# Reciprocal square roots of the mixers' norms: Ln and Exp on ScalarE replaced by Sqrt with VectorE's reciprocal, and by GpSimd's power

## The reference

```
def _l2_normalize(x):                      # RWKV keys per head of 64; GD queries and keys per head of 128
    return x * lax.rsqrt(jnp.sum(x * x, axis=-1, keepdims=True) + 1e-6)

y = ((y - mean) * lax.rsqrt(var + RW_LN_EPS)) * ln_g + ln_b      # RWKV output, per head of 64
o = _rms_norm(o, norm_g) * silu(zgate)                            # GD output, per head of 128
h = _rms_norm(h, norm_g) * sigmoid(o)                             # mLSTM output, per head of 128
```

## Time and profile before

| | us |
|---|---|
| median of three runs | 3327.88 |
| lowest, highest | 3312.94, 3331.92 |
| span of the profiled execution | 3333.3 |
| TensorE, VectorE, ScalarE, GpSimd busy | 3222.5, 2135.0, 1682.0, 610.8 |

### The profile page before, as it was taken

One profiled execution on the slowest core, in us unless ns is written; L12 is line 12 of the kernel. 1 busy time (PEld: TensorE's weight loads), 2 busy tenths in 40 slices (PEclk: granted clock), 3 DMA queues, 4 the chain that ended last, 5 costly groups with the idle time before them and its releaser, 6 DMA issues.

```text
span 3333.3 us, 51588 instructions
## 1 busy us (share of the span) xinstructions
PE 3222.5 (97%) x18431; PEld 2802.3 (84%) x18431; DVE 2135.0 (64%) x3426; ACT 1682.0 (50%) x2659; POOL 610.8 (18%) x521
## 2 busy tenths in 40 slices
PE   8999998999999999999999999999999999999998
PEld 7899897877888888888788998887878888888886
DVE  5775655776677777545568655556767777774554
ACT  5545544444655555444455565434455555554444
POOL 2000442342122212100000013324411222220000
PEclk9999997999999999999999998979999999999999
DMA  6666001113566666665556650011145665656654
GB/s 204 180 181 180 25 1 32 49 58 95 172 194 193 188 183 193 223 194 189 166 167 193 188 149 1 1 51 57 52 124 177 192 189 178 187 191 219 192 185 153
DMA packets 265208, 478.91 MB, mean 144 GB/s; under 512 B 17314, under 2 KB 81148, under 8 KB 264380
## 3 DMA queue, kind: packets, MB, share of 16 engines
q1 hardware_dynamic: 265020, 476.48, 46.4%
HBM read 474.32 MB, written 2.10 MB: 143 GB/s over the span
## 4 chain that ended last, share of the span: by engine, by line
PE 90%; DVE 5%; ACT 2%; issue 1%; DVEq 0%; ACTq 0%; POOL 0%; SPq 0%; DMA 0%; POOLq 0%
PE ps L625 89%; PE ps L629 1%; ACT L1223 1%; DVE wlo L1727 1%; DVE upair L1740 0%; ACT UA L1223 0%; DVE H L1759 0%; DVE AR L2128 0%; ACT XS L1223 0%; DVE TN L2149 0%; DVE TN L1786 0%; DVE rf L2163 0%; POOL H L562 0%; ACT whi L1223 0%; DVE XS L1776 0%
## 5 line engine op out<-in xcount | busy, mean ns | idle before, releaser
L1727 DVE TENSOR_TENSOR wlo<-ring,whi 128x1024 fp32r<-128x1024 f32 (+4 forms) x905 | 1086.3, 1217 | 693.8 <-ACT whi L1223 687.3
L625 PE MATMUL ps<-upair,whi 128*128 128x512 f32 x4032 | 1416.9, 396 | 5.8 <-DVE upair L1740 5.2
L1223 ACT ACTIVATE whi<-ring 128x1024 fp32r<-128x1024 f32 (+4 forms) x947 | 941.1, 1002 | 805.3 <-PE ps L625 752.8
L625 PE MATMUL ps<-upair,wlo 128*128 128x256 f32 x4032 | 1130.9, 280 | 0.0
L625 PEld LDWEIGHTS ps<-upair,whi 128*128 128x128 f32 x4032 | 757.4, 188 | 186.1 <-issue 5.9
L625 PEld LDWEIGHTS ps<-upair,wlo 128*128 128x128 f32 x4032 | 762.7, 189 | 0.3 <-issue 0.2
L625 PE MATMUL ps<-whi,upair 128*128 128x390 f32 (+2 forms) x1280 | 367.9, 364 | 0.0
L607 POOL TENSOR_TENSOR YB<-YB 128x1024 f32<-128x1024 f32 x22 | 125.2, 5691 | 837.9 <-DVE YB L1750 837.9
L625 PE MATMUL ps<-whi,ghi 128*128 128x512 f32 x704 | 274.4, 390 | 0.0
L625 PE MATMUL ps<-whi,glo 128*128 128x512 f32 x704 | 274.0, 389 | 0.0
L625 PE MATMUL ps<-wlo,ghi 128*128 128x512 f32 x704 | 273.9, 389 | 0.0
(11 more groups left out here) (304 smaller groups left out, 3802.6 us busy)
## 6 DMA issues: line engine op xcount, KB each, us to landing
ring<-in_w_up_dram SPq DMA_DIRECT2D x352, 512.0 KB, 3.8
ring<-in_w_down_dram SPq DMA_DIRECT2D x176, 512.0 KB, 4.2
ring<-in_w_in_dram SPq DMA_DIRECT2D x128, 384.0 KB, 3.5
ring<-in_w_out_dram SPq DMA_DIRECT2D x64, 512.0 KB, 3.8
ring<-in_w_ple_gate_dram SPq DMA_DIRECT2D x64, 512.0 KB, 4.1
ring<-in_w_in_dram SPq DMA_DIRECT2D x51, 512.0 KB, 4.4
ring<-in_w_in_dram SPq DMA_DIRECT2D x64, 390.0 KB, 3.5
ring<-in_w_in_dram SPq DMA_DIRECT2D x32, 396.0 KB, 3.4
```

Of the source, the lines that this page charges most:

```text
L625: return pe.matmul(o_, a, b, start=start, stop=stop, skip_group_check=True)
L1223: return act.activation(o_, i_, f, **kw)
L1727: v.tensor_tensor(wlo[:, slot % RING, :, 0:w], ring[:, slot % RING, :, 0:w], whi[:, slot % RING, :, 0:w].bitcast(F32), SUB).then_inc(S["lo ...
```

## The change

ScalarE takes no logarithm for a norm any more. For the RWKV keys it only copies the sums out of PSUM, at level 1, and signals `rw_rn` there; GpSimd adds epsilon and raises to the power -0.5 by a tensor_tensor with `ALU.pow` against a broadcast column of -0.5. The RWKV output norm goes to GpSimd wholly, which now waits for `rw_var`. For the GD keys ScalarE takes Sqrt, and VectorE the reciprocal of both 128x512 tiles, between its exponents and AR. For the GD and mLSTM outputs ScalarE takes Sqrt, VectorE the reciprocal of 128x4. `ready_roots` and `ready_exps` place table loads by hand: the set with Sqrt ahead of the wait for the mLSTM sums, the set with Exp behind the key norms' signal.

```diff
@@ GpSimd
+                def inverse_root(o_, i_, width, eps):
+                    pool.tensor_tensor(pst[:, 0:1], ident[:, 0:1], ident[:, 0:1], ALU.mult)
+                    pool.tensor_scalar(o_, i_, 1.0 / width, eps, ALU.mult, ALU.add)
+                    pool.drain()
+                    pool.tensor_tensor(o_, o_, epsb[:, 3:4].to_broadcast([P, o_.shape[-1]]), ALU.pow)
+                    pool.drain()
 ...
                     pool.wait_ge(S["rw_rn"], n + 1)
+                    inverse_root(ch[:, 3, :], ch[:, 3, :], 1, EPS)
                     pool.tensor_tensor(ch[:, 4, :], ch[:, 1, :], ch[:, 3, :], ALU.mult)
 ...
-                    pool.wait_ge(S["rw_rstd"], n + 1)
+                    pool.wait_ge(S["rw_var"], n + 1)
+                    inverse_root(st[:, 2, :], st[:, 1, :], 64, RW_LN_EPS)
                     pool.tensor_tensor(o4, o4, bc(st[:, 2, :], 64), ALU.mult)
@@ ScalarE
-            def rsqrt(o_, i_, scale, bias):
-                a(o_, i_, ACT.Ln, scale=scale, bias=bias)
-                act.drain()
-                return a(o_, o_, ACT.Exp, scale=-0.5)
+            def ready_roots():
+                act.preload_act_table_set("sqrt_and_friends")
+            def ready_exps():
+                act.preload_act_table_set("exp_and_friends")
+            def root(o_, i_, scale, bias):
+                return a(o_, i_, ACT.Sqrt, scale=scale, bias=bias)
 ...
-            def rw_norms(c, n, logs, exps, banks=(1, 5)):
-                if logs:
+            def rw_norms(c, n, sums, values, banks=(1, 5)):
+                if sums:
                     act.wait_ge(S["rw_ssq"], n + 1)
-                    a(ch[:, 3, :], ps[banks[0]][:, 0:T], ACT.Ln, bias=epsb[:, 0:1])
-                    if c > 1:
-                        act.wait_ge(S["rw_var"], n - 1)
-                        a(st[:, 2, :], st[:, 1, :], ACT.Ln, scale=1.0 / 64, bias=epsb[:, 1:2])
-                if exps:
-                    act.drain()
-                    a(ch[:, 3, :], ch[:, 3, :], ACT.Exp, scale=-0.5)
-                    if c > 1:
-                        a(st[:, 2, :], st[:, 2, :], ACT.Exp, scale=-0.5).then_inc(S["rw_rstd"], 1)
+                    a(ch[:, 3, :], ps[banks[0]][:, 0:T], ACT.Copy)
                     rc = rows["r_k"] + c
                     a(ch[:, 2, :], zrw[:, c, :], ACT.Copy, scale=par[:, rc:rc + 1])
                     act.drain().then_inc(S["rw_rn"], 1)
+                if values:
                     act.wait_ge(S["rw_vt"], n + 1)
 ...
-                def rw_rstd(n):
-                    act.wait_ge(S["rw_var"], n + 1)
-                    rsqrt(st[:, 2, :], st[:, 1, :], 1.0 / 64, epsb[:, 1:2]).then_inc(S["rw_rstd"], 1)
 ...
-                            else:
-                                rw_rstd(n - 1)
 ...
                     act.wait_ge(S["gd_ssq"], n + 1)
                     for j in range(2):
-                        a(mono(ewg[j], 2), ps[(7, 5)[j]][:, :], ACT.Ln, bias=epsb[:, 0:1])
-                    act.drain()
-                    for j in range(2):
-                        last = a(ewg[j], ewg[j], ACT.Exp, scale=-0.5)
+                        last = root(mono(ewg[j], 2), ps[(7, 5)[j]][:, :], 1.0, epsb[:, 0:1])
                     last.then_inc(S["gd_rn"], 1)
+                    ready_exps()
 ...
                         if src == "gd_us":
                             partial_out(ng, sg, 2)
+                            ready_roots()
                             act.wait_ge(S["ml_ss"], n + 1)
-                            rsqrt(st[:, 2, :], st[:, 1, :], 1.0 / P, epsb[:, 0:1]).then_inc(S["ml_rstd"], 1)
+                            root(st[:, 2, :], st[:, 1, :], 1.0 / P, epsb[:, 0:1]).then_inc(S["ml_rstd"], 1)
 ...
-                    rsqrt(st[:, 2, :], st[:, 1, :], 1.0 / P, epsb[:, 0:1]).then_inc(S["gd_rstd"], 1)
+                    root(st[:, 2, :], st[:, 1, :], 1.0 / P, epsb[:, 0:1]).then_inc(S["gd_rstd"], 1)
@@ VectorE
                 v.wait_ge(S[fam + "_rstd"], n + 1)
+                v.reciprocal(st[:, 2, :], st[:, 2, :])
+                v.drain()
                 v.tensor_tensor(OL, OL, bc(st[:, 2, :], P), MUL)
 ...
                     v.wait_ge(S["gd_rn"], n + 1)
+                    for j in range(2):
+                        v.reciprocal(mono(ewg[j], 2), mono(ewg[j], 2))
+                    v.drain()
                     for h in range(2):
```

More of the change, by code:

```diff
@@ L256, in trunk @@
             inv_tn1 inv_x inv_xs inv_q inv_t inv_tn inv_tq inv_tt0 inv_tt1 inv_th
-            rw_u rw_uf rw_state rw_s0 rw_pv2 rw_rf2 rw_u2 rw_uf2 rw_y rw_yc rw_var rw_rstd rw_done
+            rw_u rw_uf rw_state rw_s0 rw_pv2 rw_rf2 rw_u2 rw_uf2 rw_y rw_yc rw_var rw_done
             gd_sp gd_ln gd_gl gd_cum gd_cumc gd_exp gd_silu gd_sq gd_ssq gd_rn gd_vt gd_vtc gd_qk gd_kt gd_ktc gd_sc
@@ L437, in _ @@
             for dst, v in ((ones[:], 1.0), (one_h[:], 1.0), (ident[:], 0.0), (headones[:], 0.0), (prow, 0.0),
-                           (epsb[:, 0:1], EPS), (epsb[:, 1:2], RW_LN_EPS), (epsb[:, 2:3], 1.0)):
+                           (epsb[:, 0:1], EPS), (epsb[:, 1:2], RW_LN_EPS), (epsb[:, 2:3], 1.0), (epsb[:, 3:4], -0.5)):
                 pool.memset(dst, v)
@@ L1517, in _ @@
                     rw_pair(c, c < RC - 1)
-                rw_rstd(act.snap(L * RC + (RC - 1)))
                 def ml_pair(n2, lv):
```

## The result

| | us |
|---|---|
| median after | 3613.11 (3612.86 to 3623.09) |
| median before, measured beside it | 3329.9 (3312.94 to 3333.15) |
| ratio | 1.0871, 95% interval 1.0842 to 1.0900 |
| span of the profiled execution | 3611.1, against 3333.3 before |

The change makes the kernel 8.7% slower: +283 us, where +15 was forecast. The time lies far outside the range.

The account below looks back on a forecast made before the run. TensorE, busy 97% of the span, bounds the kernel. A layer, C 6.7 + D 6.9 + F 2.9 - B 3.0 - B's clock 5.0 - E 0.9 = +7.6; two, +15 on 3327.9: 3343 us, range 3325 to 3390.

Parts of the forecast that it names:

- A: Norms of the rwkv pairs moved to GpSimd: 13.7 us to spare, cost nothing if the wide power stays under 12 us.
- F: First rwkv pair's products: 3.8 us to spare, the added GpSimd chain costs +2.9 us a layer with the power at 5.7.
- rival 3: GpSimd's wide power is slow, costing later pairs too: 3375 us at a 15 us power, 3416 at 20; chance 0.23.
- B: Last rwkv pair: ScalarE's chain loses two loads and a Ln, -3.0 us; TensorE's clock stays up, -5.0 us, each layer.
- rival 2: TensorE's clock in the last rwkv pair falls all the same: 10 us more, 3353 us; chance 0.18.
- C: Round 0, GD key norms: two wide VectorE reciprocals, 3.3 us each, go on the path, +6.7 us a layer.
- Rivals 4 and 5: Round reciprocals: 4, streaming like ordinary operations, 3308 us, chance 0.06; 5, eight times ordinary per element, 3356 us, chance 0.07.
- D: Rounds 1 and 2: reciprocals outweigh saved loads, +2.7 us and +0.75 of clock each, +6.9 us a layer.
- E: End of round 2: VectorE's wait for ScalarE shortens, small reciprocals added, net -0.9 us a layer.
- Rest: Row-norm load behind the mixers, moved rw_var wait, last output norm and hand-placed loads: hidden or about where they were.
- Rival 6: Loads are still put before each Sqrt beside the hand-placed ones: hidden behind the reciprocals, 3343 us too; chance 0.04.

Follow-up runs that it names:

- experiment 3: Kernel before with only the RWKV output norms moved to GpSimd, with a power of 128x4; 3298.52 us, ratio 0.9921.
- experiment 6: Kernel of experiment 1 with each of VectorE's two wide reciprocals a round replaced by a product with a constant; 3312.33 us, ratio 0.9969.
- experiment 1: Changed kernel with the 128x256 power of the RWKV key norms replaced by a same-shape GpSimd product; 3339.73 us, ratio 1.0039.
- experiment 2: Kernel before with only the GD and mLSTM part of the change (Sqrt, VectorE reciprocals, hand-placed loads); 3357.64 us, ratio 1.011.

## Why the prediction was wrong, step by step

**A and F failed by the price of the wide power.** The prediction bounded it by 0.73 and 5.7 us, the engine's longest row of any kind, and took 5.7; it is 41.27. The longest row of another operation is no bound for an operation that the trace doesn't have, and the range went by it. With 5.7 us step A came out at nothing and F at 2.9 us a layer; measured, TensorE stands 26.4 to 27.8 us at the coefficient product of each of pairs 1 to 3, and the first pair starts 27.6 us late. The power was the only term with nothing comparable in the trace; that called for more than 0.23 on rival 3, and for an upper end of the range that doesn't stop at 17 us.

**Rival 3's mechanism was right, its two terms not quite.** Its rule (F grows as the power less 2.8 us, A costs three times what exceeds 12.7) gives 3353, 3422 and 3586 for powers of 10.7, 20.9 and 41.3 us; measured were 3363, 3464 and 3613. The rule let the first pair's products take as long as before, but behind a long power GpSimd's products no longer run beside VectorE and take 10.7 us (372.52 to 383.22, against 16.3 before, 332.30 to 348.56). So at the product that the forecast took, the second direction's AR,KB, TensorE comes 30.9 us late and not 38.5. The forecast had also overlooked the coefficient product, which waits for YB: GpSimd had that at 340.31 before, 10.1 us ahead of TensorE, and has it at 377.87 in after, which gives the measured 27.6. For A the waits came near what was said (26.8, 26.4 and 27.8 us against 28.6, and 1.5 more for each direction's KB and AR). What the rule left out is the clock: 14.5 and 12.6 us a layer in after. Whether "Cost nothing if the wide power stays under 12 us" holds is not shown: at 10.7 us the waits of pairs 1 to 3 are the old 0.41 us, one layer lost time to its clock and the other didn't, and the kernel as a whole was some 21 us slower than without the power.

**B held.** The first two loads of the chain are gone: ScalarE comes straight to the gates (time line), and the stretch behind it (row of stretches) is at full clock.

```profile
642.94 0.25 ACT L1232 ACTIVATE gx<-gx 128x48 f32<-128x48 f32 x1
643.24 1.28 ACT L1232 ACT_TABLE_LOAD   x1
```

```profile
639.00:649.00 10.00, 9.53 (x80) 9.15 (x81) 6.95 (x16) 6.09 (x12) 5.20 (x9) 1.00 0.01 2
```

These answer to the earlier trace rows, where two loads and a clock of 0.50 stood. From TensorE's level 1 product to the sums of round 0 it is 41.35 us in after and 49.79 before: -8.4, forecast -8.0. The same stretch is 41.3 to 42.1 us in experiments 3 and 6 and in layer 1 of experiment 1. So rival 2 falls: the clock stays up behind the gap. That the whole pair gained 13.4 us in layer 0 of experiment 1 is luck and no part of B: 5 us of it are a higher clock ahead of the sums, which experiment 6 doesn't show again. In after the pair as a whole gained nothing, since its start, behind the wait, lost 9.7 us at half clock.

**C held.** The reciprocals are 3.31 us each, the wait for AR in round 0 is 10.72 us (forecast 10.7), the stretch +6.8 (forecast +6.7, experiment 2: +6.6).

```profile
695.49 6.54 DVE L2127 RECIPROCAL UA<-UA 128x512 f32<-128x512 f32 x2
```

(Time line of VectorE, round 0.) By experiment 6 an ordinary operation there would give back 5.5 us. The slope from 2 to 4 elements a lane was a good guide to 512. Rivals 4 and 5 fall. The repeat count of 8 that the Trainium skill gives for the reciprocal (VectorE: DVE Perf Modes, "First, the fixed hardware budget"), taken as eight times the ordinary 1.03 ns an element, makes an estimate of 4.4 us; measured is 3.31, or six times.

**D held in its sum, not in its parts.** +3.8 a round, forecast 3.45 (2.7 + 0.75). The forecast gave GpSimd's split 0.5 us against VectorE; it took 1.8 (2.48 against 0.69 at L1805). For that the chain left earlier: VectorE's wait for its factor was 0.39 us and ended at 772.0, 1.5 us behind the sums, where the forecast had 2.0.

The time line of round 1 in after, GpSimd and VectorE:

```profile
771.84 2.35 POOL L565 TENSOR_TENSOR wlo<-ring,whi 128x1024 fp32r<-128x1024 f32 x1 [20.64 <-DVE st L1798]
...
772.27 2.48 DVE L1805 TENSOR_TENSOR heads<-heads,st 128x512 f32<-128x512 f32 x1
...
785.98 0.42 DVE L2131 TENSOR_TENSOR AR<-Z,UA 128x256 f32<-128x256 f32 x1
```

**E** is -0.7 in layer 0 (forecast -0.9). **Rest**: nothing of it shows. **Rival 6** falls, with 42 loads.

**The sum without A and F** was C + D + E + B = 6.7 + 6.9 - 0.9 - 8.0 = +4.7 a layer, 3337. Experiment 1 is that case: 3340, with 3334 to 3350 as its interval. So the forecast named the small cause of a slower kernel and sized it about right, with some luck in the total, and mis-sized the large one: the reciprocals cost some tenths of a per cent, the power 8%.

## What to carry to other kernels

An operation that the trace doesn't show has no upper bound in it, however long the longest row: where such an operation sits in front of the bounding engine, time it alone first, and give its unknown price most of the range. A delay on another engine can cost more than the wait that it makes, through TensorE's clock, so compare busy time and granted clock over a whole stage; but compare them in several executions and layers of the same code first, since here the clock alone moved one stage by 5 us. Before replacing functions to save table loads, see whether one set holds them all (90 loads became 32 by two hand-placed loads a layer), and then look at what the earlier engine now runs beside.

## What the runs showed of the hardware

- GpSimd's tensor_tensor power in float32 takes 0.159 us an element of a lane: 1.14 us for 4 columns, 10.67 for 64, 20.87 for 128, 41.27 for 256; the product of 256 takes 0.72.
- VectorE's reciprocal takes 0.172 us for 128x4 and 3.31 for 128x512, the same alone and beside GpSimd's weight split. Ordinary operations that meet that split end only some 0.6 us behind its end: a 128x512 product takes 2.15 to 2.48 us instead of 0.69, two 128x512 scalings 2.22 instead of 0.74.
- TensorE worked at 0.50 of its clock for the 20 us behind a stop of 27 us.
- Its clock also falls with nearly no idle time: to 0.66 over 22.7 us with 0.31 us idle in experiment 3's layer 1, where layer 0 of the same kernel kept 1.00. The 22 us ahead of round 0's sums had 0.56 before, 0.60 in experiment 6, and 0.92 and 0.55 in the two layers of experiment 1, whose code there is experiment 6's.
